# Low parts of the weights on VectorE alone, and the modulation's products moved from GpSimd to TensorE

## The reference, cut to what matters

```python
c_act = jax.nn.silu(c)
for i in range(DEPTH):                       # DEPTH = 2
    mod = c_act @ mod_w[i] + mod_b[i]        # (1, 1024) @ (1024, 6144)
    sh_m, sc_m, g_m, sh_f, sc_f, g_f = jnp.split(mod[:, None, :], 6, axis=-1)
    h = rms_norm(x, norm_mix_pre[i]) * (1.0 + sc_m) + sh_m
    ...
```

## Time and profile before

| | |
|---|---|
| runs | 2698.08 us median of 3 (2697.8 to 2703.37) |
| profiled execution, its span | 2699.4 us |
| PE busy, of the span | 2440.6 us, 90% |
| DVE busy | 1856.6 us, 69% |
| ACT busy | 1194.6 us, 44% |
| POOL busy | 1029.9 us, 38% |
| bytes moved | 405.77 MB, mean 150 GB/s |

### The profile page before, as it was taken

How to read it: one execution, slowest core, us unless ns; L and a number is a source line. 1 busy time by engine, 2 the same in 40 slices (tenths; PEclk the granted TensorE clock), 3 DMA queues, 4 the chain that set the end, 5 groups by cost and what they waited for, 6 DMA issues and landing times.

```text
span 2699.4 us, 45800 instructions
## 1 busy us (share of the span) xinstructions
PE 2440.6 (90%) x17794; PEld 2347.4 (87%) x17794; DVE 1856.6 (69%) x2446; ACT 1194.6 (44%) x1720; POOL 1029.9 (38%) x501
## 2 busy tenths in 40 slices
PE   7998887998999999887898899898789799897998
PEld 7998777998998999877798899798677799897997
DVE  5667899766666666899975677573734488756555
ACT  5444342254444444443235444435323365543654
POOL 3655443054665566443125466221100122221222
PEclk9999898599999999999679999899655799998999
DMA  6665434045665565533214566343200155443552
GB/s 249 211 221 187 148 126 133 1 164 172 210 228 192 177 227 210 182 135 133 78 59 168 165 224 219 115 158 124 93 9 0 65 178 185 148 149 101 184 182 101
DMA packets 110412, 405.77 MB, mean 150 GB/s; under 512 B 12256, under 2 KB 12384, under 8 KB 109920
## 3 DMA queue, kind: packets, MB, share of 16 engines
q1 hardware_dynamic: 96192, 352.33, 38.5%
q0 software_dynamic: 13824, 50.34, 5.8%
q10 hardware_dynamic: 288, 1.57, 0.2%
HBM read 403.14 MB, written 1.05 MB: 150 GB/s over the span
## 4 chain that ended last, share of the span: by engine, by line
PE 66%; DVE 20%; issue 8%; POOL 3%; ACT 2%; DMA 0%; POOLq 0%; DVEq 0%; SPq 0%; ACTq 0%
PE bank L537 64%; DVE arena L1461 6%; DVE w_lo L1304 4%; PE bank L649 2%; POOL w_lo L467 1%; DVE arena L1506 1%; POOL mod_acc L502 1%; POOL mod_w_buf L494 1%; DVE arena L1511 1%; DVE rinv L1338 1%; DVE work L1342 1%; DVE work L1374 0%; DVE arena L1700 0%; DVE arena L1515 0%; DVE arena L1509 0%
## 5 line engine op out<-in xcount | busy, mean ns | idle before, releaser
L537 PE MATMUL bank<-h_hi,w_hi 128*128 128x256 f32 (+1 forms) x4016 | 1184.4, 295 | 124.2 <-DVE w_lo L1304 64.2
L537 PE MATMUL bank<-h_lo,w_hi 128*128 128x256 f32 (+1 forms) x4016 | 1160.8, 289 | 0.0
L537 PE MATMUL bank<-h_hi,w_lo 128*128 128x256 f32 (+1 forms) x4016 | 1159.4, 289 | 0.0
L467 POOL TENSOR_TENSOR w_lo<-w_raw,w_hi 128x1024 fp32r<-128x1024 f32 x221 | 551.7, 2496 | 1577.5 <-ACT w_hi L982 1576.9
L982 ACT ACTIVATE w_hi<-w_raw 128x1024 fp32r<-128x1024 f32 x663 | 700.1, 1058 | 784.7 <-PE bank L537 782.4
L537 PEld LDWEIGHTS bank<-h_hi,w_hi 128*128 128x128 f32 x4016 | 794.3, 198 | 144.2 <-DVE w_lo L1304 57.4
L1304 DVE TENSOR_TENSOR w_lo<-w_raw,w_hi 128x1024 fp32r<-128x1024 f32 x442 | 688.4, 1564 | 331.7 <-ACT w_hi L982 328.0
L537 PEld LDWEIGHTS bank<-h_lo,w_hi 128*128 128x128 f32 x4016 | 797.3, 199 | 5.7 <-issue 5.5
L537 PEld LDWEIGHTS bank<-h_hi,w_lo 128*128 128x128 f32 x4016 | 795.8, 198 | 0.0
L1461 DVE SCALAR_TENSOR_TENSOR arena<-arena,vecs 128x256 f32<-128x256 f32 x520 | 316.8, 672 | 0.0
L537 PE MATMUL bank<-hid_hi,w_hi 128*128 128x256 f32 x1056 | 297.9, 282 | 3.1 <-DVE hid_lo L1390 3.1
(11 more groups left out here) (205 smaller groups left out, 2093.2 us busy)
## 6 DMA issues: line engine op xcount, KB each, us to landing
w_raw<-weights SPq DMA_DIRECT2D x663, 512.0 KB, 3.4
mod_w_buf<-mod_w POOLq DMA_DIRECT2D x96, 512.0 KB, 4.0
tabs<-shape_tables SPq DMA_DIRECT2D x1, 1746.0 KB, 14.6
work<-v_bias ACTq DMA_DIRECT2D x2, 768.0 KB, 5.1
x<-x_fm SPq DMA_DIRECT2D x1, 1024.0 KB, 4.9
out_fm<-x SPq DMA_DIRECT2D x1, 1024.0 KB, 3.9
vecs<-vectors SPq DMA_DIRECT2D x1, 712.0 KB, 8.3
tabs<-shape_tables SPq DMA_DIRECT2D x1, 65.0 KB, 4.8
```

The costliest lines, as they stand in the source:

```text
L467: nc.gpsimd.tensor_tensor(w_lo[:, SPLIT - 1, :], w_raw[:, n % RAW, :], w_hi[:, SPLIT - 1, :].bitcast(F32), ALU.subtract).then_inc(lo_ready ...
L537: ins = pe.matmul(o, lhs, rhs, start=start, stop=stop, skip_group_check=share)
```

## The change

POOL does no arithmetic any more: it only issues the loads of `mod_w`, now with four buffers and up to four tiles ahead. DVE writes every low part. PE forms the modulation itself: each of the 96 tiles gives eight blocks of 128 by 128, each block is the stationary operand and one column of `c_act` moves, and the eight tiles of a part accumulate in PSUM. `mod_part` and `mod_vector` stay at their places.

```diff
 RAW = 6
+MOD_BUF = 4
...
-        mod_acc = sb("mod_acc", 2, D_MODEL)
-        mod_w = sb("mod_w_buf", 2, TILE)
+        mod_w = sb("mod_w_buf", MOD_BUF, TILE)
...
         def _(pool):
             w = Count()
-            state = {"tile": SPLIT - 1}
-
-            def low_part():
...
-            def two_parts(part):
...
+            for n in range(DEPTH * MOD_PARTS * KT):
+                if n >= MOD_BUF:
+                    was = n - MOD_BUF
+                    if was % KT == KT - 1:
+                        pool.wait_ge(mod_col_full, was // KT + 1)
+                    else:
+                        pool.wait_ge(mod_w_used, was // KT * (KT - 1) + was % KT + 1)
+                pool.dma_start(mod_w[:, n % MOD_BUF, :], mod_in[n]).then_inc(mod_w_full[n % MOD_BUF], 16)
...
                 p = state["part"]
                 state["part"] += 1
-                pe.wait_ge(mod_acc_ready, w.next(mod_acc_ready))
-                for c in range(KT):
-                    mm(bank[b][:, c:c + 1], mod_acc[:, p % 2, c * P:(c + 1) * P], tab("one"),
-                       sig=mod_col_full if c == KT - 1 else None)
+                if p == 0:
+                    pe.wait_ge(c_ready, w.next(c_ready))
+                for kt in range(KT):
+                    n = p * KT + kt
+                    pe.wait_ge(mod_w_full[n % MOD_BUF], w.next(mod_w_full[n % MOD_BUF], 16))
+                    if kt == 0 and p:
+                        pe.wait_ge(mod_ready, w.next(mod_ready))
+                    for c in range(KT):
+                        mm(bank[b][:, c:c + 1], mod_w[:, n % MOD_BUF, c * P:(c + 1) * P], c_act[:, kt:kt + 1],
+                           (kt, c) == (0, 0), kt == KT - 1,
+                           (mod_col_full if kt == KT - 1 else mod_w_used) if c == KT - 1 else None, share=True)
...
                 while state["split"] <= min(upto, N_TILES - 1):
                     n = state["split"]
-                    if n % SPLIT == SPLIT - 1:
-                        w.skip(hi_ready, 1)
-                    else:
-                        dve.wait_ge(hi_ready, w.next(hi_ready))
-                        v.tensor_tensor(w_lo[:, n % SPLIT, :], w_raw[:, n % RAW, :],
-                                        w_hi[:, n % SPLIT, :].bitcast(F32), ALU.subtract
-                                        ).then_inc(lo_ready[n % SPLIT], 1)
+                    dve.wait_ge(hi_ready, w.next(hi_ready))
+                    v.tensor_tensor(w_lo[:, n % SPLIT, :], w_raw[:, n % RAW, :],
+                                    w_hi[:, n % SPLIT, :].bitcast(F32), ALU.subtract
+                                    ).then_inc(lo_ready[n % SPLIT], 1)
                     state["split"] += 1
```

More of the change, by code:

```diff
@@ L392, in build @@
         c_ready = sem("c_activated")
-        mod_w_full = [sem(f"mod_weight_full{i}") for i in range(2)]
-        mod_acc_ready = sem("mod_products_ready")
+        mod_w_full = [sem(f"mod_weight_full{i}") for i in range(MOD_BUF)]
+        mod_w_used = sem("mod_weight_used")
         mod_col_full = sem("mod_columns_in_psum")
@@ L460, in _ @@
             w = Count()
-            state = {"tile": SPLIT - 1}
-            def low_part():
[L465 to L474, removed]
-                else:
-                    src = mod_in[bass.ds(part * KT + kt, 1)].rearrange("a p w -> (a p) w")
-                pool.dma_start(mod_w[:, kt % 2, :], src).then_inc(mod_w_full[kt % 2], 16)
@@ L524, in _ @@
-            w.turned(left // 2)
-            if left % 2:
-                low_part()
+            for n in range(DEPTH * MOD_PARTS * KT):
[6 more added lines that the diff above has]
+                pool.dma_start(mod_w[:, n % MOD_BUF, :], mod_in[n]).then_inc(mod_w_full[n % MOD_BUF], 16)
```

## The result

The changed kernel takes 2854.26 us, the median of four runs (2850.48 to 2856.05), beside 2699.39 us for the kernel before (four runs, 2697.8 to 2703.37). The ratio is 1.057, with a 95% interval of 1.055 to 1.058: 5.7% slower. 2857 us was forecast. The profiled execution has a span of 2848.7 us, 149.3 more than before; the sum had +158.4.

What follows compares the result with a forecast made beforehand. The prediction took the kernel to be bound by TensorE's stream, with stretches where VectorE sets the pace. Terms 64.4 + 39.2 + 31.4 + 27 - 6 + 2.4 = +158.4 on a 2699.4 us span gave 2857 us named, range 2785 to 2915.

Steps and rivals of the forecast that it cites:

- The burst B: Each modulation part on TensorE: 128 instructions, most at half clock and a pitch near 0.18 us, 21.5 us.
- Norm places: Parts 3, 5, 9 and 11: the norm is ready behind the part's burst; +16.1 us each, +64.4 together.
- recurrence's +2.4: Block 2's recurrence: VectorE, alone on the path, makes two low parts that GpSimd made before; +2.4 us.
- Places 4 and 10: Final norms: mod_vector stands ahead of final_norm on VectorE, so the part's added time is exposed; 2 x 19.6 = +39.2 us.
- Places 2 and 8: Parts with columns on both sides: added time counted whole, 39.2 us, less TensorE's low-part waits of 5.1 and 2.7; +31.4.
- The mixers' first stretch: Block 1's two mixers, parts 0, 1, 6, 7: later gates and a wait inside, less faster VectorE steps; +13.5 us each.
- The first ffn: First ffn: long low parts on the chain become 1.2 us, 0 to 15 us come back; -6 us taken.
- Transfers: Loads of the modulation's tiles into the buffers: no wait of TensorE at the median.
- The rest: Stages outside the other terms, such as attention heads with no part and no tile: 0.
- the first: Rival: the clock stays at 2.4 GHz in the parts, 15.2 us each; +70, 2768 us; chance 0.13.
- The second: Rival: 128-row weight loads slower when cold, 26.2 us a part, 2913 us, or late transfers, 2875; chance 0.11.
- The third: Rival: VectorE's relief decides, with warm parts wholly in TensorE's gaps in the mixers; 2690 us; chance 0.03.

Runs made afterwards that it cites:

- 64-column version: The changed kernel with 64 equal columns of c_act moved for each block instead of one; 2744.0 us, one run.
- one-tile version: The changed kernel with only the last of each part's eight modulation tiles loaded and multiplied; 2607.21 us, ratio 0.966.
- heads' versions: The changed kernel with modulation tiles spread behind the attention units' scores, moving 64 columns or one; 2919.58 and 2919.53 us.
- run with few blocks: The changed kernel with one of eight blocks multiplied in each part's first seven tiles, all tiles still loaded; 2716.93 us, ratio 1.006.
- late reads: The changed kernel with 64 equal columns and mod_vector behind final_norm or the first token pair's result; 2721.77 us, ratio 1.008.

## Why the prediction was right, point by point

The prediction was right: 2857 us forecast, 2854.26 measured, and the cause is the one named, TensorE's cold bursts, shown by the 64-column version (110 us less with most of the clock held) and by the one-tile version (243 us for 84 of the 96 tiles). But the nearness of the number is luck. The stages' forecasts miss by up to 11.7 us, and it is their errors that cancel: the mixers' first stretches come out 23 us below the forecast, the bursts' other places 19 us above it, the rest 5 below. The sum for the span was 9.1 us too high, and the median stands 5.6 us above the profiled span here, not 1.3 below, which hides most of that. By terms of the sum:

- **The burst B** was forecast at 21.5 us and takes 23.0 to 24.8 with its last instruction. Step mis-sized: the pitch of one column at half clock, carried on from 64 and 15 columns to 0.18 us. It is 0.213: at this clock the pitch does not fall with fewer columns (the heads' versions have the same with 64 and with one). The line ran through two shapes, 128 rows at 64 columns and 64 rows at 15; the row with 128 rows, 0.225, alone was nearer. With it 3.0 + 103 x 0.213 would be 24.9; it is a little less because 27 to 45 instructions, not 25, go out at full clock, 0.1 us apart. This adds 1.5 to 3.3 us in each of 12 places, some 29 in all.
- **Norm places**: +16.1 forecast, +19.4, +21.3 and +17.8 measured at 3, 5 and 9; B's error is most of it. The stage of place 11 also holds the recurrence's +2.4: 18.5 forecast, +15.4 measured. There the first column behind the burst comes 18.3 us later against the root, and some 3 us are made up further on in the mixer; what makes them up stays open. **Places 4 and 10**: +19.6 forecast, +21.2 and +21.0. VectorE's wait was put at about 20 us there and is 26.7 and 25.8.
- **Places 2 and 8**: +15.7 forecast, +21.9 and +18.1. The burst costs what B measures: against the one-tile version the stage is 22.3 and 21.7 us longer. What failed is the credit for TensorE's waits on low parts, 5.1 and 2.7 us: with GpSimd quiet the one-tile version gains only 0.4 (205.0 to 204.6) and 3.6 us (207.6 to 204.0).
- **The mixers' first stretch**: +13.5 forecast, +2.3 and +1.8 measured. This is where the sum was wrong by 23 us. The gates start 18.3 us later against the root (15.6 forecast, and B's error), as argued. But the gate pairs took 41.5 us, not 46.5 (251.3 to 292.8): two steps at TensorE's 5.76 us, as forecast, and five at VectorE's 5.96, not 7.0. VectorE's eight taps take 3.25 us together, 0.41 each, since one starts before the last has ended; I took 0.48 from the duration of a single one. A q step is 7.5 us instead of 8.7. The token pairs took 26.4 instead of 30.0 for the same reason. VectorE therefore comes to the second part earlier and waits 15.05 us instead of 11.6. So the step that failed is VectorE's pace, priced by durations where starts count. The forecast of the first attention unit, 14 us later, failed in its sign by the same term and by leaving out the first ffn's -6.
- **The first ffn**: -6 forecast, -6.6 measured. **Transfers**: no wait of TensorE, as forecast; the run with few blocks shows that they would hold a part at some 12 us.
- **The rest**: 0 forecast beyond the recurrence, -4.3 measured.

These two rows show the taps' true pace, TensorE's step being hidden behind it (timeline of VectorE after, two q steps, 7.48 us apart; x8 are the eight taps):

```profile
324.23 3.25 DVE L1407 SCALAR_TENSOR_TENSOR arena<-arena,vecs 128x256 f32<-128x256 f32 x8
...
331.71 3.25 DVE L1407 SCALAR_TENSOR_TENSOR arena<-arena,vecs 128x256 f32<-128x256 f32 x8
```

Of the rivals, the first (the clock stays, 2768 us) did not come; the version with 64 columns, in which it mostly stays, takes 2744.0, so its price was some 24 us too high, although that version also waits 7.0 us for transfers; in the mixers' first stretches it stands 22.5 us below this rival's forecast, again the mixers' error. The Trainium skill's rule weighed there ("TensorE: Matmul & The Clock Gate", What's actually happening), that activity releases the throttle, can't be read off the profile's busy time: TensorE was busy throughout, and the granted clock went from 1.00 to 0.50. So the measurement decided. The second (2913) had the better pitch, but its transfers' waits did not come. The third named the faster side's mechanism rightly, and the one-tile version shows it at 92 us; it could not decide here, since B was 24 and not 15 us, and even with bursts of 14 to 19 us and late reads it did not.

What the forecast did not see is that low parts on VectorE alone are no gain by themselves: it credited the relief to GpSimd doing nothing, which is right, and did not ask what GpSimd's products alone would do. The experiments left one thing open: why 64 columns hold the clock in most bursts of 128 instructions and not in the heads, where bursts of 16 or 32 stand between the heads' own matmuls.

## What to carry to other kernels

Before a product of a vector with a matrix is given to TensorE, count its weight loads and price them at half clock: the products of 96 tiles, 427 us of GpSimd's time, lay on an engine that was no bound (38% busy), and 84 of these tiles cost 243 us on the one that was. When GpSimd slows VectorE, look first at when it does so: with all low parts on VectorE, GpSimd's products back to back lost 4.6%, at the old pace they gained 0.7%, and under stretches in which TensorE hides VectorE 2.2%, where moving them to TensorE lost 5.7%. And price a run of like operations from the distance of their starts, not from the duration of one.

## What the runs showed of the hardware

- The bursts of 128 back-to-back instructions with one moving column, TensorE busy all the time by the profile, go from a granted clock of 1.00 to 0.50 within about 5 us of their start. The first of them with 64 equal columns holds 1.00 and is 9 us shorter, though it does 64 times the work; in five of the twelve there is a wait, and part of the burst goes at half clock.
- At a granted clock of 0.50 the pitch of such an instruction is 0.213 us with one column and with 64 alike (32 in 6.90 us), and in the heads 64 columns do not keep the clock up: it goes from 1.00 to 0.50 within 10 us and stays there.
- Two-source operations of VectorE on 128x256 last 477 ns each by the profile, but eight in a row take 3.25 us, 0.41 each: one starts before the last has ended.
- The same 180 multiplications and additions on GpSimd make 143 us of difference by their spacing alone (2822.27 against 2679.02 us).
